# Gated DeltaNet on one core: the 128x128 triangular inverses joined by 32x32 and 64x64 products instead of full 128x128 ones

## The reference, cut to what matters

```
lower = where(strict, (k * beta) @ k.T * decay, 0)
a_mat = eye(C) + lower
sol = triangular_solve(a_mat, rhs, lower=True, unit_diagonal=True)
qk = (q @ k.T) * decay
step: v_new = u - w @ S;  out = q_dec @ S + qk @ v_new;  S = S * exp(gl) + k_dec.T @ v_new
```

## Time and profile before

| | us |
|---|---|
| median of 3 runs | 1505.37 (1505.32 to 1506.95) |
| profiled execution, its own time | 1504.56 |
| its span, first to last instruction | 1502.8 |
| PE busy in the span | 1461.3 (97%) |
| PEld / DVE / ACT / POOL busy | 1235.9 / 598.6 / 560.5 / 649.2 |

### The profile page before, as it was taken

How to read it: one execution, slowest core, us unless ns; L and a number is a source line. 1 busy time by engine, 2 the same in 40 slices (tenths; PEclk the granted TensorE clock), 3 DMA queues, 4 the chain that set the end, 5 groups by cost and what they waited for, 6 DMA issues and landing times.

```text
span 1502.8 us, 19558 instructions
## 1 busy us (share of the span) xinstructions
PE 1461.3 (97%) x7595; PEld 1235.9 (82%) x7595; DVE 598.6 (40%) x1105; ACT 560.5 (37%) x1063; POOL 649.2 (43%) x299
## 2 busy tenths in 40 slices
PE   6999999999999999999999999999998999999997
PEld 6988888658889888888889878879988988888886
DVE  3641002363274400233135545995756540024223
ACT  5232233353252222232233676754835222123231
POOL 5244343443554444353445244364435344434441
PEclk9999999999999999999999999999999999999999
DMA  6322323301323222323223132211013123232321
GB/s 233 108 85 86 109 84 112 140 1 40 111 77 121 90 99 87 110 84 108 88 84 120 56 113 84 85 56 57 30 57 127 57 85 111 86 111 84 112 84 56
DMA packets 66699, 136.32 MB, mean 91 GB/s; under 512 B 3648, under 2 KB 4160, under 8 KB 66240
## 3 DMA queue, kind: packets, MB, share of 16 engines
q1 hardware_dynamic: 64016, 125.90, 25.4%
q10 hardware_dynamic: 2608, 9.38, 1.7%
HBM read 133.16 MB, written 2.11 MB: 90 GB/s over the span
## 4 chain that ended last, share of the span: by engine, by line
PE 90%; DVE 4%; ACT 2%; POOL 1%; DMA 1%; issue 1%; SPq 0%; ACTq 0%; DVEq 0%
PE bank L426 27%; PE bank L427 27%; PE bank L428 26%; PE bank L608 2%; POOL side_lo L313 1%; PE bank L812 1%; PE bank L825 1%; PE bank L678 1%; PE bank L594 1%; PE bank L722 1%; DVE mix L1500 1%; DMA w_raw<-in_ret_w_in_dram 1%; DVE act_lo L1526 1%; DVE gv L1714 1%; PE bank L473 1%
## 5 line engine op out<-in xcount | busy, mean ns | idle before, releaser
L313 POOL TENSOR_TENSOR w_lo<-w_raw,w_hi 128x1024 fp32r<-128x1024 f32 (+1 forms) x218 | 520.2, 2408 | 680.1 <-ACT w_hi L959 680.0
L959 ACT ACTIVATE w_hi<-w_raw 128x1024 fp32r<-128x1024 f32 x210 | 210.9, 1054 | 461.5 <-PE bank L428 417.1
L426 PE MATMUL bank<-act_hi,w_hi 128*128 128x512 f32 (+1 forms) x832 | 299.7, 360 | 9.8 <-DVE act_lo L1526 7.9
L428 PE MATMUL bank<-act_hi,w_lo 128*128 128x512 f32 (+1 forms) x832 | 297.9, 358 | 0.0
L427 PE MATMUL bank<-act_lo,w_hi 128*128 128x512 f32 (+1 forms) x832 | 297.8, 358 | 0.0
L427 PE MATMUL bank<-w_lo,hid_hi 128*128 128x512 f32 x480 | 189.0, 394 | 0.0
L426 PE MATMUL bank<-w_hi,hid_hi 128*128 128x512 f32 x480 | 188.2, 392 | 0.0
L426 PEld LDWEIGHTS bank<-act_hi,w_hi 128*128 128x128 f32 x832 | 158.3, 190 | 34.8 <-DVE act_lo L1526 9.2
L428 PE MATMUL bank<-w_hi,hid_lo 128*128 128x512 f32 x480 | 186.4, 388 | 0.0
L1633 DVE TENSOR_TENSOR relu_sq<-relu 128x512 f32<-128x512 f32 x64 | 48.6, 759 | 328.6 <-ACT relu L982 328.0
L428 PEld LDWEIGHTS bank<-act_hi,w_lo 128*128 128x128 f32 x832 | 158.2, 190 | 22.5
(11 more groups left out here) (260 smaller groups left out, 2185.5 us busy)
## 6 DMA issues: line engine op xcount, KB each, us to landing
w_raw<-in_mlp_w_up_dram SPq DMA_DIRECT2D x32, 1024.0 KB, 5.4
w_raw<-in_mlp_w_down_dram SPq DMA_DIRECT2D x32, 1024.0 KB, 5.0
w_raw<-in_ret_w_in_dram SPq DMA_DIRECT2D x24, 1024.0 KB, 5.1
w_raw<-in_gdn_w_in_dram SPq DMA_DIRECT2D x16, 1024.0 KB, 5.2
w_raw<-in_ret_w_out_dram SPq DMA_DIRECT2D x8, 1024.0 KB, 5.0
gains<-in_norm_gains_dram ACTq DMA_DIRECT2D x8, 512.0 KB, 5.9
w_raw<-in_gdn_w_out_dram SPq DMA_DIRECT2D x4, 1024.0 KB, 5.1
resid<-in_x_dram SPq DMA_DIRECT2D x4, 512.0 KB, 9.2
```

Of the source, the lines that this page charges most:

```text
L313: done = nc.gpsimd.tensor_tensor(LO[slot][:, kt, :], w_raw[:, raw, kt, :], HI[slot][:, kt, :].bitcast(F32), ALU.subtract)
L426: pe.matmul(dst, sta_hi, mov_hi, start=first, stop=False)
L428: return pe.matmul(dst, sta_lo, mov_hi, start=False, stop=last)
L959: act.activation(HI[raw if slot is None else slot][:, kt, :], w_raw[:, raw, kt, :], ACT.Copy)\
```

## The change

The 32x32 and 64x64 blocks are now multiplied by themselves, at their places in the array, instead of inside 128x128 matrices.

- Small joins (32 into 64): for each unit and both pairs of diagonal blocks, `small_halves` makes the 32x32 product of `neg_l_t`'s block with `upright`; ScalarE copies 32 partitions by 512 out at a time (`small_halves_out`), 16 units in one instruction; `small_corners` multiplies by `flipped`. For the first pair a third product with the operands swapped gives the same corner upright, which makes the transposes of `inv_t` unnecessary. All 8 heads are served with one batch behind the other before the next step.
- Wide joins (64 into 128): `wide_halves` and `wide_corners`, one 64x64 product each per unit, on the upper or lower half of the partitions. The upright 64x64 block lies in the new tiles `pair`, put together by GpSimd (zeros, two diagonal blocks) and ScalarE (`upright_join`).
- The products of q and the key transposes stand between these steps on TensorE, and the q products use other banks (`Q_BANK`).
- `inv`, the mask `join` and its load, the memset of `inv`, the seeding copies from `upright` to `inv`, and all copies of turned inverses are gone. VectorE copies corners with plain copies. The first memset of `inv_t` waits only for the first half of the last z group.
- VectorE makes `upright` right behind `flipped`; the columns that scale q (`q_columns`) come after the joins, and so does ScalarE's square root for them.

Counted in products: before, 128 products of 128x128 and 48 transposes of 128x128 for the inverses; now 160 products of 32x32 and 64 of 64x64. The 24 q products and 32 key transposes of this stage are the same in number.

```diff
@@ -381,15 +389,22 @@
             for c in range(GDN_Z[1], GDN_OUT[1]):
                 low_side(c, c % 2, 2)
 
+            pool.wait_ge(chunk_used, GDN_Z[2] + 2)
+            pool.memset(inv_t[:, batch_units(0), :], 0.0).then_inc(sem("inv_t_cleared"), 1)
             pool.wait_ge(bank_full, 4 * GDN_OUT[0])
-            for half in range(2):
-                pool.memset(inv_t[:, half * UNITS // 2:(half + 1) * UNITS // 2, :], 0.0).then_inc(sem("inv_t_cleared"), 1)
+            pool.memset(inv_t[:, batch_units(1), :], 0.0).then_inc(sem("inv_t_cleared"), 1)
             pool.wait_ge(sem("inv_t_cleared"), 2)
-            pool.wait_ge(sem("blocks_flipped"), 1)
-            for i in range(P // BLOCK):
-                q = slice(i * BLOCK, (i + 1) * BLOCK)
-                late = slice(UNITS // 2, UNITS)
-                nc.gpsimd.tensor_copy(inv_t[q, late, q], flipped[q, late, :]).then_inc(sem("late_seeded"), 1)
+            pool.wait_ge(sem("blocks_flipped"), 2)
+            for batch in range(2):
+                pool.memset(pair[batch][QUARTERS[0], :, BLOCK:2 * BLOCK], 0.0).then_inc(sem("pair_seeded"), 1)
+                pool.wait_ge(sem("pair_seeded"), 3 * batch + 1)
+                for i in range(2):
+                    nc.gpsimd.tensor_copy(pair[batch][QUARTERS[i], :, small_cells(i)],
+                                          upright[QUARTERS[i], batch_units(batch), :]).then_inc(sem("pair_seeded"), 1)
+                pool.wait_ge(sem("pair_seeded"), 3 * batch + 3)
+            for q in QUARTERS:
+                nc.gpsimd.tensor_copy(inv_t[q, batch_units(1), q], flipped[q, batch_units(1), :])\
+                    .then_inc(sem("late_seeded"), 1)
             pool.wait_ge(sem("late_seeded"), 4)
             def q_products(first, last):
 
                 for h in range(first, last):
-                    if h >= 4:
-                        pe.wait_ge(emptied, 4 * (GDN_OUT[0] - 1) + h - 3)
-                    products(h, h, gq).then_inc(sem("unit_prods"), 1)
+                    if h >= 6:
+                        pe.wait_ge(sem("unit_scaled"), h - 3)
+                    elif h >= 2:
+                        pe.wait_ge(emptied, 4 * (GDN_OUT[0] - 1) + h - 1)
+                    products(h, Q_BANK[h], gq).then_inc(sem("unit_prods"), 1)
             def delta_rule():
-                q_products(2, GH)
...
+                def units_in(batch):
+                    return range(batch * UNITS // 2, (batch + 1) * UNITS // 2)
+                def small_halves(batch):
+                    if batch:
+                        pe.wait_ge(sem("unit_scaled"), 2)
+                    for k in range(2):
+                        near, far = QUARTERS[2 * k], QUARTERS[2 * k + 1]
+                        for i, u in enumerate(units_in(batch)):
+                            done = pe.matmul(bank[2 * batch + k][far, small_cells(i)], neg_l_t[near, u, far],
+                                             upright[near, u, :], start=True, stop=True)
+                        done.then_inc(sem("half_made"), 1)
+                def small_corners(batch):
+                    for k in range(2):
+                        near, far = QUARTERS[2 * k], QUARTERS[2 * k + 1]
+                        pe.wait_ge(sem("half_out"), 2 * batch + k + 1)
+                        for i, u in enumerate(units_in(batch)):
+                            done = pe.matmul(bank[2 * batch + k][near, small_cells(i)], half_prod[far, u, :],
+                                             flipped[far, u, :], start=True, stop=True)
+                        done.then_inc(sem("corner_made"), 1)
+                        if k == 0:
+                            for i, u in enumerate(units_in(batch)):
+                                done = pe.matmul(bank[2 * batch][far, small_cells(i)], flipped[far, u, :],
+                                                 half_prod[far, u, :], start=True, stop=True)
+                            done.then_inc(sem("upright_made"), 1)
+                def wide_halves(batch):
+                    pe.wait_ge(sem("pair_seeded"), 3 * (batch + 1))
+                    pe.wait_ge(sem("upright_joined"), batch + 1)
+                    for k in range(2):
+                        pe.wait_ge(sem("joined"), 2 * batch + k + 1)
+                        for i in range(2 * TT):
+                            v = 2 * TT * k + i
+                            done = pe.matmul(bank[2 * batch + k][FAR, pair_cells(i)],
+                                             neg_l_t[NEAR, batch * UNITS // 2 + v, FAR], pair[batch][NEAR, v, :],
+                                             start=True, stop=True)
+                        done.then_inc(sem("half_made"), 1)
+                def wide_corners(batch):
+                    pe.wait_ge(sem("late_seeded" if batch else "seeded"), 4)
+                    for k in range(2):
+                        pe.wait_ge(sem("half_out"), 4 + 2 * batch + k + 1)
+                        for i in range(2 * TT):
+                            v = 2 * TT * k + i
+                            done = pe.matmul(bank[2 * batch + k][NEAR, pair_cells(i)], pair[batch][FAR, v, :],
+                                             inv_t[FAR, batch * UNITS // 2 + v, FAR], start=True, stop=True)
+                        done.then_inc(sem("corner_made"), 1)
+                def turn_keys(first):
+                    if first:
+                        pe.wait_ge(sem("unit_scaled"), GH)
+                    for r in range(4):
+                        if not first:
+                            pe.wait_ge(sem("k_faded"), r + 1)
+                        turn(gk, first + r, 4 + r, "k_turned")
+                pe.wait_ge(sem("blocks_flipped"), 2)
+                small_halves(0)
+                small_halves(1)
+                q_products(2, 6)
+                small_corners(0)
+                small_corners(1)
+                q_products(6, GH)
+                wide_halves(0)
+                wide_halves(1)
+                turn_keys(4)
+                wide_corners(0)
+                wide_corners(1)
+                turn_keys(0)
...
-                if gi == 7:
-                    act.wait_ge(sem("kq_x_made"), 2)
-                    act.activation(ct[:, 3, :], ct[:, 1, :], ACT.Sqrt).then_inc(sem("kq_rooted"), 1)
...
+            def small_halves_out(batch):
+                for k in range(2):
+                    far = QUARTERS[2 * k + 1]
+                    act.wait_ge(sem("half_made"), 2 * batch + k + 1)
+                    act.activation(half_prod[far, batch_units(batch), :],
+                                   bank[2 * batch + k][far, :].rearrange("p (u c) -> p u c", c=BLOCK), ACT.Copy)\
+                        .then_inc(sem("half_out"), 1)
...
+            small_halves_out(0)
+            small_halves_out(1)
             act.wait_ge(sem("inv_t_cleared"), 1)
-            act.wait_ge(sem("blocks_flipped"), 1)
-            soon = slice(0, UNITS // 2)
-            for i in range(P // BLOCK):
-                q = slice(i * BLOCK, (i + 1) * BLOCK)
-                act.activation(inv_t[q, soon, q], flipped[q, soon, :], ACT.Copy).then_inc(sem("seeded"), 1)
-            act.wait_ge(sem("blocks_flipped"), 2)
-            for i in range(P // BLOCK):
-                q = slice(i * BLOCK, (i + 1) * BLOCK)
-                act.activation(inv[q, :, q], upright[q, soon, :], ACT.Copy).then_inc(sem("upright_seeded"), 1)
-            act.wait_ge(sem("upright_seeded"), 4)
+            for q in QUARTERS:
+                act.activation(inv_t[q, batch_units(0), q], flipped[q, batch_units(0), :], ACT.Copy)\
+                    .then_inc(sem("seeded"), 1)
+            upright_join(0)
+            upright_join(1)
...
+            wide_halves_out(0)
+            wide_halves_out(1)
+            act.wait_ge(sem("kq_x_made"), 2)
+            act.activation(ct[:, 3, :], ct[:, 1, :], ACT.Sqrt).then_inc(sem("kq_rooted"), 1)
...
+            scale_products(0, 6)
+            corner_copies(0)
+            corner_copies(1)
+            scale_products(6, GH)
+            fade_keys(1)
+            wide_copies(0)
+            wide_copies(1)
+            fade_keys(0)
+            q_columns()
```

More of the change, by code:

```diff
@@ L30 @@
 BLOCK = 32
-LEVELS = [32, 64]
 CK = 4
@@ L870, in state_step @@
                         pe.wait_ge(sem("k_faded"), GH)
-                        pe.wait_ge(sem("joined"), step)
                     for r in range(4):
@@ new lines, in corner_copies @@
+            def corner_copies(batch):
+                dve.wait_ge(sem("inv_t_cleared"), batch + 1)
+                for k in range(2):
+                    near, far = QUARTERS[2 * k], QUARTERS[2 * k + 1]
+                    dve.wait_ge(sem("corner_made"), 2 * batch + k + 1)
+                    dve.tensor_copy(inv_t[near, batch_units(batch), far],
+                                    bank[2 * batch + k][near, :].rearrange("p (u c) -> p u c", c=BLOCK))\
+                        .then_inc(sem("joined"), 1)
```

143 lines of the change are left out of this document (47 added, 96 removed).

## The result

| | us |
|---|---|
| median after, 13 runs | 1492.58 (1489.74 to 1502.96) |
| median before, 13 runs beside them | 1505.87 (1504.81 to 1507.87) |
| ratio, with its 95% interval | 0.992 [0.9902, 0.9938] |
| profiled execution after: its time, span, mean granted clock | 1499.99, 1498.3, 0.986 |

The change makes the kernel faster by 0.8%; the interval excludes 1. The forecast was 1488.5 within 1485.5 to 1502. But the 13 runs spread over 13 us, where those of before spread over 3, and the time roughly follows the mean granted TensorE clock of the run: 1490.25 at 0.994, 1492.58 at 0.991, 1495.5 at 0.988, 1499.99 at 0.986. So the profiled execution is one of the worst, and shows what the others have less of.

What follows compares the result with a forecast made beforehand. The stage was taken as bound by the number and length of TensorE records: 28.1 us against 45.1, a gain of 17.0; 1504.56 - 17.0 = 1487.6, the median 0.8 higher, forecast 1488.5, range 1485.5 to 1502.

Steps and rivals of the forecast that it cites:

- The price of a small record: TensorE's new products: 0.0322 us per 32-column record and 0.0587 per 64-column one, 10.3 and 7.5 us in all.
- The line through 128 and 512 columns: Record price on TensorE extrapolated from two sizes: 0.00083 us a column plus 0.0058; chance 50%, own range 1486 to 1492.
- rivals 1 (the floor): Small TensorE records cost 0.05 us at 32 columns and 0.07 at 64; gain 9.8, 1495.6 us; chance 21%.
- 2 (load and stream one after the other): Weight load and stream at one array place don't overlap: 0.062 and 0.117 us a record; gain 0, 1505.4; chance 9%.
- 3 (0.1116 whatever the size): Every TensorE record costs 0.1116 us whatever its size; 15.2 us longer, 1520.6 us; chance 9%.
- The sum: TensorE's stage from z group to solve: 8.9 + 10.3 + 7.5 + 1.4 = 28.1 us against 45.1, a gain of 17.0.
- changes of shape: TensorE switching between 128, 32 and 64 columns: 8 changes at about 0.09 us lost each, 0.7 us.
- changes of place: Some 8 moves within the array inside the small joins, price unknown, booked at 0.7 us; zero and 0.16 each as ends.
- rival 4: Granted TensorE clock falls to 1.2 GHz over small products: 1494.5 us if over small corners only, up to 1506; chance 11%.
- The start: VectorE has `upright` ready at 1005.3, before TensorE comes free at 1006.31: 1 us to spare, no wait counted.
- The other engines: ScalarE, VectorE and GpSimd copies, `pair` pieces and scaling stay hidden under TensorE's work, with covers 0.3 to 10 us thick.
- The q columns: VectorE's q columns (1.8 us), directly ahead of its first state copy in the solve, may make it 0.3 us late.

Runs made afterwards that it cites:

- e4_small_spread: The changed kernel with only the small joins spread among the q products of heads 2 to 5; wide steps unchanged; 1488.93 us, ratio 0.9889.
- e7_alternate_wide: Nearly e4_small_spread's order, but small products alternate between places and the second batch's wide halves alternate with the first's wide corners; 1486.42 us.
- e9_no_wait: e7_alternate_wide with VectorE's scaling of heads 6 and 7 between the two batches of corner copies and q products earlier; 1484.59 us, ratio 0.9852.
- e5_old_start: e4_small_spread with VectorE's q columns and scaling of heads 0 and 1 back ahead of the second transpose, ScalarE's square root back too; 1500.67 us.
- e1_spread: The changed kernel with both small and wide steps mixed with full-size q products and key transposes; 1490.41 us, ratio 0.990.
- e0_again: The changed kernel run again unchanged, against the kernel before; 1500.04 us over 7 runs, ratio 0.9948.
- e10_columns: e9_no_wait with VectorE's q columns and ScalarE's square root early, the columns behind the scaling of heads 0 and 1; 1482.06 us, ratio 0.9835.

## Why the prediction came out as it did

- **The price of a small record**, the step with most in it, was right: 0.0302 us measured for 0.0322 forecast, and 0.0605 for 0.0587. The line through 128 and 512 columns holds down to 32 within 6%. With that rivals 1 (the floor), 2 (load and stream one after the other) and 3 (0.1116 whatever the size) are out. The floor is even lower: 0.012 where places alternate.
- **The sum** was near: 28.1 us forecast, 27.96 in `e4_small_spread`, the same products at full clock. A part of that order, though, is not the changed kernel's: full-size products stand at more places between small ones, at some 0.2 us a group (8 q records take 1.09 us there, by 0.1116 they would take 0.89), as two changes of shape at 0.09 say. For the changed kernel's own order at full clock I estimate 26.7 us: 7.63 for halves and q products and 5.56 for the small corners from the profile after (6.11 less half of the 1.1 us at the low clock), and 13.51 for the rest from `e4_small_spread`. So the sum was about 1.4 us too long, half of it the changes of place.
- **Changes of place** were booked at 0.09 each, 0.7 us in all. They are free, and more: records at different places overlap. The Trainium skill (TensorEngine Tiling (Array Packing), Key Properties) has it that a change of tile doesn't drain the engine; the starts 0.01 us apart at the seams agree.
- **The clock** is where the forecast fell short. The forecast expected a granted clock of 1.00; rival 4 is what happened, in both profiles and, by the mean clocks, in nearly all of the 20 runs of the changed kernel (0.986 to 0.995; before 0.994 to 0.997). It had 11%. The argument against it was that a gap of 2.2 us left the clock alone; but here no gap is needed, and one gap that left it alone doesn't show that gaps do: the clock fell at waits of 2.20 us in `e7_alternate_wide` and 2.12 in `e9_no_wait`. The price was also set by the wrong stretch: I let the clock be low for the small corners (6 us) or for all joins (17.8), while it fell late and stayed down over full-size work as well, 10.7 us in the profiled execution and 3 to 4 in the median of the first 13 runs, if 1492.58 against the 1488.93 of `e4_small_spread` is put on it. In the 7 further runs the same kernel had a median of 1500.04, so the size of this loss isn't a property of the kernel alone; whether the chip makes the difference isn't shown.
The Trainium skill (TensorE: Matmul & The Clock Gate, Part 1) speaks of how busy TensorE has been; TensorE is busy for 6.11 of 6.11 us in the stretch in which its clock falls, so busy time as the profile counts it doesn't decide here.
- **The start** was right: no gap, and `e5_old_start` shows the 2.6 us that the new order of VectorE saves. The memset beside the block products cost nothing: it ran from 995.18 to 997.00, beside the end of the product of 900 elements and the sum over it, and that product took 2.88 us (2.86 before).
- **The other engines** kept up: the copies of halves, the `pair` pieces, the corner copies and the key scaling never hold TensorE in the profile after, where the low clock gives them more time, nor in `e4_small_spread`, where it is busy for 27.96 of 27.96 us. The q columns were thought 0.3 us late and weren't. These covers hold for this order and length: in the order of `e1_spread` (29.7 us) the scaling of the last heads was 1.03 us late, and at some 22 us (`e9_no_wait`) the columns were late.
- **The median**: 1492.58 lies in the range and 4.1 us above the forecast, just outside the 1486 to 1492 that the line had for itself. That it is so near is in part luck: a sum some 1.4 us too long and a clock taken as 1.00 err in opposite directions, and the upper end of the range was drawn for dearer records, which didn't come, and not for the clock. No execution at the median was profiled, so that the clock makes the whole difference is argued from the mean clocks (0.991 for that run, 0.994 to 0.997 in `e4_small_spread`).

## What to carry to other kernels

A small product costs by its columns down to 32, and 0.4 to 0.6 of that where its neighbours use other places in the array: order such products unit by unit across places, not place by place. Don't let small products run for several us together; put full-size products between them. Count a wait of TensorE of 2 us or more as more than its length, ahead of small products above all, since the clock may fall at it. Judge by several runs and their granted clocks, since one execution of the same kernel can show 0 or 12 us of the loss. When a stage shrinks by half, look again at what the other engines do beside it, since their work now falls on other neighbours.

## What the runs showed of the hardware

- The clock fell from 2.4 to 1.2 GHz with TensorE 100% busy, in streams of 32x32 records (0.67 of full speed in a stretch of 4 us with 108 of them, 0.50 in the next), and not in streams of 64x64 records (3.87 us twice) or 128x128 transposes. Why it falls is open.
- Of four waits of TensorE of 2.1 to 2.6 us in this stage and right behind it, the clock fell at three: within one of 2.20 us (`e7_alternate_wide`), 1.9 us behind one of 2.12 with only full-size products around (`e9_no_wait`), and 1.9 us behind one of 2.57 ahead of small ones (`e5_old_start`). At the one of 2.2 us in the kernel before it stayed at 1.00.
- Once down it stayed at 0.50 for about 3.4 us (`e9_no_wait`, and the first fall in `e0_again`) up to 27 us (profile after) and 48 us (`e5_old_start`), with TensorE busy throughout.
- Records at different places overlap: 32x32 ones 0.0177 us apart at two places and 0.012 at three, 64x64 ones 0.031 at two; at one place 0.0302 to 0.032 and 0.0605.
- GpSimd can hold a tiny VectorE step until its own instruction ends, a memset included, and in `e9_no_wait` across two instructions in a row (3.90 us beside two of 2.35). In `e10_columns` VectorE and GpSimd:

```profile
1007.83 1.74 DVE L1821 TENSOR_SCALAR col<-ct 128x32 f32<-128x32 f32 x1
```

```profile
1007.73 1.80 POOL L395 MEMSET inv_t<- 128x2048 f32 x1 [10.88 <-PE bank L443]
```

The step (0.18 us elsewhere) ended at 1009.57, the memset at 1009.53. In the profile after, the product of 900 elements and the sum over it, beside the clearing of the other half of `inv_t`, were not slowed.
The Trainium skill (SBUF — State Buffer, Who interferes with whom) has both: it says that tensor_scalar can enter a mode in which it contends with GpSimd, and it lets a sum, and a product of two inputs beside a memset, go on. The trace agrees, with 1.74 us for the one and 2.88 against 2.86 for the other.
